# A layout of its own for the second expert pass in the weight ring of a two-layer decoder kernel

## The reference

```
logits = t @ w_router
top_v, top_i = lax.top_k(logits, TOP_K)            # 2 of 8
top_p = jax.nn.softmax(top_v, axis=-1)
combine = sum(one_hot(top_i, 8) * top_p[..., None], axis=1)
for e in range(8):
    out = out + combine[:, e:e+1] * ((silu(t @ w_gate[e]) * (t @ w_up[e])) @ w_down[e])
```

## Time and profile before

| what | us |
|---|---|
| median of 3 runs | 1017.01 (1016.84 to 1018.2) |
| the profiled execution | 1018.07 |
| its span | 1016.3 |
| TensorE busy in the span | 1001.5 (99%) |
| DMA, mean rate over the span | 250 GB/s (252.93 MB read) |

### The profile page before, as it was taken

The page is one execution under the profiler, slowest core; times in us unless marked ns, Lnnn a source line. Parts: engine busy times, 40 slices in busy tenths (PEclk is TensorE's granted clock), DMA queues, the critical chain, the costliest instruction groups (busy, mean ns, idle before and its releaser), DMA issues.

```text
span 1016.3 us, 22250 instructions
## 1 busy us (share of the span) xinstructions
PE 1001.5 (99%) x9679; PEld 863.3 (85%) x9679; DVE 592.1 (58%) x991; ACT 401.6 (40%) x627; POOL 13.6 (1%) x57
## 2 busy tenths in 40 slices
PE   8999999999999999999999999999999999999995
PEld 8999999999999999999999999996566566566552
DVE  6667766577677565376577665755542542542443
ACT  6735655535544344357356565352102002002012
POOL 3000000000000000000000000000000000000000
PEclk9999999999999999999999999999999999999998
DMA  7453543555555465465435437989979999999993
GB/s 282 160 159 104 198 146 111 187 200 189 176 187 186 144 217 201 150 232 166 163 107 188 154 99 263 394 326 405 405 305 414 410 411 414 413 408 414 414 408 139
DMA packets 56017, 255.40 MB, mean 251 GB/s; under 512 B 6609, under 2 KB 6641, under 8 KB 55922
## 3 DMA queue, kind: packets, MB, share of 16 engines
q1 hardware_dynamic: 55346, 252.94, 67.2%
q10 hardware_dynamic: 576, 1.07, 0.3%
HBM read 252.93 MB, written 1.05 MB: 250 GB/s over the span
## 4 chain that ended last, share of the span: by engine, by line
PE 85%; SPq 9%; DMA 3%; issue 1%; ACT 1%; DVE 1%; DVEq 0%
PE ps L1721 24%; PE ps L1716 18%; PE ps L1717 18%; PE ps L1718 18%; SPq L611 8%; PE ps L1710 2%; PE ps L1711 2%; PE ps L1712 2%; DMA e_ring<-in_experts 2%; DMA raw<-in_dense 1%; PE ps L1926 1%; ACT w_hi L754 0%; ACT squared L759 0%; PE ps L1744 0%; PE ps L1898 0%
## 5 line engine op out<-in xcount | busy, mean ns | idle before, releaser
L1075 DVE TENSOR_TENSOR w_lo<-raw,w_hi 128x1536 fp32r<-128x1536 f32 (+2 forms) x156 | 247.5, 1605 | 122.0 <-ACT w_hi L754 121.6
L754 ACT ACTIVATE w_hi<-raw 128x1536 fp32r<-128x1536 f32 (+2 forms) x156 | 209.2, 1362 | 145.2 <-DMA raw<-in_dense 142.5
L1716 PE MATMUL ps<-hT_hi,w_hi 128*128 128x256 f32 (+1 forms) x816 | 231.7, 284 | 1.6 <-DVE w_lo L1217 1.1
L1717 PE MATMUL ps<-hT_lo,w_hi 128*128 128x256 f32 (+1 forms) x816 | 230.4, 282 | 0.0
L1718 PE MATMUL ps<-hT_hi,w_lo 128*128 128x256 f32 (+1 forms) x816 | 229.6, 281 | 0.0
L1721 PE MATMUL ps<-e_ring,xe 128*32 128x352 f32 (+2 forms) x2480 | 186.5, 459 | 0.0
L1721 PEld LDWEIGHTS ps<-e_ring,xe 128*32 128x32 f32 x2480 | 109.8, 110 | 73.0 <-issue 32.3
L1716 PEld LDWEIGHTS ps<-hT_hi,w_hi 128*128 128x128 f32 (+1 forms) x816 | 152.2, 186 | 5.2 <-issue 2.6
L1717 PEld LDWEIGHTS ps<-hT_lo,w_hi 128*128 128x128 f32 (+1 forms) x816 | 152.3, 187 | 0.4
L1718 PEld LDWEIGHTS ps<-hT_hi,w_lo 128*128 128x128 f32 (+1 forms) x816 | 152.3, 187 | 0.4
L1717 PE MATMUL ps<-h_lo,w_hi 128*128 128x256 f32 x352 | 99.2, 282 | 0.0
(11 more groups left out here) (313 smaller groups left out, 1427.9 us busy)
## 6 DMA issues: line engine op xcount, KB each, us to landing
e_ring<-in_experts SPq DMA_DIRECT2D x124, 704.0 KB, 15.6
raw<-in_dense SPq DMA_DIRECT2D x112, 768.0 KB, 4.3
e_ring<-in_experts SPq DMA_DIRECT2D x88, 512.0 KB, 14.5
raw<-in_dense SPq DMA_DIRECT2D x42, 512.0 KB, 3.5
e_ahead<-in_experts SPq DMA_DIRECT2D x4, 704.0 KB, 9.1
raw<-in_dense SPq DMA_DIRECT2D x3, 544.0 KB, 4.9
raw<-in_dense SPq DMA_DIRECT2D x2, 272.0 KB, 4.2
x<-in_x SPq DMA_DIRECT2D x2, 256.0 KB, 4.5
```

The lines of the kernel that those rows point to most:

```text
L754: act.activation(slot(n, "hi", k), slot(n, "raw", k), ACT.Copy).then_inc(hi_done, 1)
L1075: dve.tensor_tensor(slot(n, "lo", k), slot(n, "raw", k), slot(n, "hi", k).bitcast(F32), ALU.subtract).then_inc(lo_done, 1)
L1716: pe.matmul(out, wh, hi, start=first, stop=False, skip_group_check=True)
L1717: pe.matmul(out, wh, lo, start=False, stop=False, skip_group_check=True)
```

## The change

The second pass gets a layout of its own, as the first has. `e_first_place` now takes the pass as its first argument (0 or 1) and names a buffer as well as a place.

- Pieces 0, 1 and 2 of the second pass go to the bottom of the first chunk, into the 5120 numbers that the first pass leaves empty (three large pieces take 4224 of them).
- Pieces 3 and 4 go to `e_ahead`, which held pieces 24 and 25 of the first pass.
- Pieces 5 to 23 go to the usual places of pieces 0 to 18.
- From piece 24 on, all go to their usual places.
- `e_first_before(i, u)` now returns the count of `e_used` itself: it looks through all earlier pieces, of this pass and the one before, for the last that lay in the same place.
- SyncE's program for passes 0, 1 and 2 is written out with constant waits, and its loop starts with the fourth pass. For the third pass the waits come to the same counts as before.
- TensorE reads the second pass's pieces from the new places (`turn` is passed through `hidden`, `down_main`, `down_over` and `down`). Which matmuls there are, and in which order, does not change.

```diff
+def e_first_place(i, u):
+
+    gate_up, size = 4 * 2 * KQ, 2 * HALF_E
+    shift = len(AHEAD) * size // D
+    if i == 0 and u in AHEAD:
+        return "ahead" + str(AHEAD.index(u) // 2), AHEAD.index(u) % 2 * size, size
+    if i == 0 and 24 <= u < gate_up:
+        return ("ring",) + e_place(u - len(AHEAD))
+    if i == 0 and u >= gate_up:
+        at = CHUNK_AT[0] + size * (gate_up - len(AHEAD) - 24) + D * (u - gate_up)
+        return ("ring",) + ((at, D) if at + D <= CHUNK_AT[0] + CHUNK else e_place(u - shift))
+    spare = shift * D // size
+    if i == 1 and u < spare:
+        return "ring", e_place(len(E_UNITS) - 1)[0] + size * u, size
+    if i == 1 and u < spare + 2:
+        return "ahead0", (u - spare) * size, size
+    if i == 1 and u < 24:
+        return ("ring",) + e_place(u - spare - 2)
+    return ("ring",) + e_place(u)
+
+def e_first_before(i, u):
+
+    buffer, at, size = e_first_place(i, u)
+    out = 0
+    for j in range(i + 1):
+        for v in range(u if j == i else len(E_UNITS)):
+            other, a, n = e_first_place(j, v)
+            if buffer == other and a < at + size and at < a + n:
+                out = max(out, j * E_GROUPS + E_GROUP[v] + 1)
+    return out
...
             for u in range(24 + len(AHEAD), len(E_UNITS)):
-                sp.wait_ge(e_used, E_GROUP[e_first_before(u)] + 1)
-                expert_load(u, (0, 1), first=True)
+                sp.wait_ge(e_used, e_first_before(0, u))
+                expert_load(u, (0, 1), 0)
             sp.wait_ge(route_ready, 1)
...
-            experts = [sp.value_load(ids[0:1, 2 + e:3 + e], min_val=0, max_val=NE - 1) for e in range(2)]
-            for u in range(len(E_UNITS)):
-                sp.wait_ge(e_used, E_GROUP[e_first_before(u)] + 1 if u < 24 else E_GROUPS + E_GROUP[e_before(u)] + 1)
-                expert_load(u, experts)
-            with sp.Fori(2, iters) as i:
+            for i in range(1, 3):
+                experts = [sp.value_load(ids[0:1, 2 * i + e:2 * i + e + 1], min_val=0, max_val=NE - 1) for e in range(2)]
+                for u in range(len(E_UNITS)):
+                    sp.wait_ge(e_used, e_first_before(i, u))
+                    expert_load(u, experts, i)
+            with sp.Fori(3, iters) as i:
```

More of the change, by code:

```diff
@@ L532, in load_of, with e_unit @@
             return loaded[n % RING], 16 * (n // RING + 1)
-        def e_unit(u, first=False):
+        def e_unit(u, turn=None):
             _, _, _, k, _, c = E_UNITS[u]
[L537 to L542, removed]
+            buffer, at, size = ("ring",) + e_place(u) if turn is None else e_first_place(turn, u)
+            home = {"ring": e_ring, "ahead0": e_ahead, "ahead1": eb["e_ahead2"]}[buffer]
+            return home[:, at:at + size].rearrange("p (k c) -> p k c", k=k)
         def proj_bank(n):
@@ L606, in load, with expert_load @@
                 sp.dma_start(unit(n, "raw", k, w), src).then_inc(load_of(n)[0], 16)
-            def expert_load(u, experts, first=False):
+            def expert_load(u, experts, turn=None):
                 which, e, k0, k, c0, c = E_UNITS[u]
                 src = block_of(t["experts"][experts[e]], expert_at[which, k0, k, c0, c], k, c)
-                sp.dma_start(e_unit(u, first), src).then_inc(loaded_e[u // 2], 16)
+                sp.dma_start(e_unit(u, turn), src).then_inc(loaded_e[u // 2], 16)
             free_later = {name: units for units, name in E_FREE_LATER}
@@ L2084, in quads, with hidden @@
                 return ins
-            def hidden(half, q, i, first=False):
+            def hidden(half, q, i, turn=None):
                 u = (half * KQ + q) * 4
-                units = [e_unit(u + n, first) for n in range(4)]
+                units = [e_unit(u + n, turn) for n in range(4)]
                 ks = (2 * q, 2 * q + 1)
@@ L2125, in slot_scales, with down_unit, down_main, down_over @@
                 ins.then_inc(scale_filled, 1)
-            def down_unit(k, e, first=False):
-                return e_unit(2 * KQ * 4 + 2 * k + e, first)[:, 0, :]
+            def down_unit(k, e, turn=None):
+                return e_unit(2 * KQ * 4 + 2 * k + e, turn)[:, 0, :]
             def down_ready(k, i):
                 expert_ready(2 * KQ * 4 + 2 * k, i)
-            def down_main(k, h, first=False):
+            def down_main(k, h, turn=None):
                 cols = slice(h * HALF, (h + 1) * HALF)
-                ins = quads(5 + h, HALF, ehT[:, k, :], [down_unit(k, e, first)[:, cols] for e in range(2)], k == 0, k == FET - 1)
+                ins = quads(5 + h, HALF, ehT[:, k, :], [down_unit(k, e, turn)[:, cols] for e in range(2)], k == 0, k == FET - 1)
                 if k == FET - 1:
                     ins.then_inc(y_filled, 1)
-            def down_over(ks, first=False):
+            def down_over(ks, turn=None):
                 for k in ks:
                     for g in range(4):
-                        ins = plain(ps[g * OV:(g + 1) * OV, 7, 0:QUARTER], ehT2[:, k, :], down_unit(k, 0, first)[:, g * QUARTER:(g + 1) * QUARTER],
+                        ins = plain(ps[g * OV:(g + 1) * OV, 7, 0:QUARTER], ehT2[:, k, :], down_unit(k, 0, turn)[:, g * QUARTER:(g + 1) * QUARTER],
                                     k == 0, k == FET - 1)
@@ L2149, in k_pair, with down @@
                 return range(2 * q, min(2 * q + 2, FET))
-            def down(q, i, first=False):
+            def down(q, i, turn=None):
                 for k in k_pair(q):
@@ L2157, in down, with first_half @@
                     for h in range(2):
-                        down_main(k, h, first=first)
+                        down_main(k, h, turn=turn)
                 if q == TURNED // 2:
                     pe.wait_ge(turn1_read, i * 2 + 2)
-                down_over(k_pair(q), first).then_inc(e_used, 1)
-            def first_half(i, first=False):
-                if not first:
+                down_over(k_pair(q), turn).then_inc(e_used, 1)
+            def first_half(i, turn=None):
+                if turn != 0:
                     pe.wait_ge(y_split, i * 3 + 3)
@@ L2171, in first_half, with second_half @@
                     slot_scales(i)
[L2172 to L2175, removed]
+                hidden(0, 0, i, turn)
+                hidden(0, 1, i, turn)
+                hidden(0, 2, i, turn)
+                if turn == 0:
                     pe.wait_ge(scale_known, 1)
                     slot_scales(i)
-                hidden(0, 3, i)
-            def second_half(i, first=False):
+                hidden(0, 3, i, turn)
+            def second_half(i, turn=None):
                 for q in range(KQ):
-                    hidden(1, q, i, first)
+                    hidden(1, q, i, turn)
                 pe.wait_ge(scale_ready, i + 1)
@@ L2190, in _, with full_pass @@
             pe.wait_ge(moe_zero, 1)
-            def full_pass(i, first=False):
-                first_half(i, first)
-                second_half(i, first)
+            def full_pass(i, turn=None):
+                first_half(i, turn)
+                second_half(i, turn)
                 for q in range(DQ):
-                    down(q, i, first)
+                    down(q, i, turn)
                 pe.wait_ge(sel_ready, i + 2)
@@ L2200, in _ @@
             for i in range(STATIC):
-                full_pass(i, i == 0)
+                full_pass(i, i)
             pe.wait_ge(iters_ready, 1)
```

## The result

The changed kernel takes 1019.56 us (median of 16 runs, 1017.92 to 1020.84) against 1017.33 (16 runs, 1016.4 to 1018.76): 2.2 us slower by the medians, ratio 1.0021 with the interval 1.0014 to 1.0029. The forecast was slower by 1.4 us, to 1018.4 us. The profiled execution has a span of 1017.1 us against 1016.3.

A forecast was written before the change was run, and what follows sets the result against it. The end was taken to follow the DMA stream's last landing, with at most 1.7 us to gain. New holes of 8.1 + 0.4 to 0.9 less 7.0, or +0.4 by landings, gave 1017.0 + 1.4 = 1018.4 us, range 1016.6 to 1019.9.

The forecast's parts named there:

- What bounds the kernel: Expert passes: the end follows the last DMA landing; earlier loads could gain at most 1.7 us, later ones cost fully.
- What the change gives: Start of the second pass: first issues come at about 732.6, and the 7.0 us DMA hole closes.
- What it takes: Second pass: piece 24 waits for count 16, not 15, a new 8.1 us hole; piece 27 adds 0.4 to 0.9.
- The sum: Whole kernel: holes opened less the hole closed, taken as +1.4 us, between +0.4 and +2.0.
- by landings: Pieces 24 and 27 of the second pass: landing times move by −0.2 and +0.4 us, so the end by +0.4.
- by the mean of the engines: DMA stream of the second pass: 8.1 + 0.4 to 0.9 − 7.0 = 1.5 to 2.0 us later.
- Edits at nothing: Other buffer for two DMAs, TensorE's weight reads, the third pass's counts and `ids` reads: no cost.
- The signs: Changed kernel's profile: empty windows at 779 to 785, last landing at 1000.5 to 1002.1, fourth TensorE down 26 to 28 us.
- The kept gain: Second pass: the old hole closes and no new one opens; −1.7 us, 1015.3 us; chance 4%.
- Landings rule: End of the loads: the slow engines are those forgiven at the hole; +0.2 to +0.7 us, about 1017.5; chance 28%.
- the forecast's own case: Whole kernel: slower by +0.8 to +2.0 us, 1017.8 to 1019.0 us; chance 46%.
- the rival with more holes: Second pass from piece 24: the queue runs short two or three times; +2.2 to +3.0 us, about 1019.6; chance 20%.

The follow-up runs named there:

- the longer wait: Kernel before, but piece 24 of the second pass waits for count 17 and not 15; ratio 1.0077 (1.0059 to 1.0095).
- the run with fewer bytes: Kernel before, but only the first half of pieces 24 to 31 of the second pass is loaded; ratio 0.9983 (0.9974 to 0.9992).
- the layout without the gap: Changed kernel with other places for pieces 24 to 53 of the second pass, and later counts in the third; ratio 0.9986, median 1015.8 us.
- the waits alone: Kernel before, but pieces 24 to 47 of the second pass wait for the changed kernel's counts; ratio 1.0024 (1.0013 to 1.0035).
- the late start: Changed kernel, but piece 0 of the second pass waits for count 8 again and not 6; ratio 1.0026 (1.0016 to 1.0036).
- the extra buffer: Kernel before, with pieces 3 and 4 of the second pass loaded to and read from another buffer, counts unchanged; ratio 0.9998 (0.9989 to 1.0007).

## Why the prediction was right, and where it was off

- *What bounds the kernel.* Right. TensorE's three first passes did not change in any run but the one with the longer wait, and the end moved with the DMA stream. The cap of 1.7 us is 1.8 us in the traces, and the run with fewer bytes shows it, which had 6.9 us of work less; the layout without the gap only just reaches it. One reading was incomplete: the 27th slice has 326 GB/s in the rows of before, so the 30th isn't the only exception. In windows of that trace the engines move 17 GB/s from 680 to 685 us, and are near 410 from 691 to 736. The queue is full from there to the hole at 737 us, so this earlier pause may well cost time too; no run tries it. It is there in the changed kernel too (39 GB/s from 680 to 685), so it doesn't bear on the difference.
- *What the change gives.* Right: the early issues came at 731.87, which is 732.7 on the time of the trace before, for a forecast of 732.6, and the hole of 7.0 us closed.
- *What it takes.* Right in place and cause: piece 24 waits for count 16, with all behind it. Its size was 7.8 us for 8.1, and 0.8 us at piece 27 for 0.4 to 0.9; no further hole opened. The run with the waits alone shows that this is the whole loss, within the noise.
- *The sum.* This is the term that was mis-sized. I took 1.4 us between +0.4 (by landings) and +2.0 (by the mean of the engines). The end by landings was wrong, though the two landings that it rests on came out as forecast: piece 24 landed at 789.3 on the time of the trace before (784.31 + 4.1 + 0.85) and piece 27 at 795.3. They are the first pieces behind each hole, and only these are early for their turn. Piece 28, right behind, landed 11.3 us after its issue at 785.16 before, at 796.5; in the changed kernel 6.4 us after its issue at 790.85, at 798.1 with the 0.85 us:

```profile
DMA to landing us min/median/max: 11.3/11.3/11.3
...
DMA to landing us min/median/max: 6.4/6.4/6.4
```

  That is 1.6 to 1.7 us later, not 0.4. The longer wait says the same: 6.8 us of hole became 6.9 us of time. The trace of the changed kernel has +1.6 us, and the medians 2.2, with an interval of 1.4 to 2.9 us. The three kernels with these waits have +1.6, +1.7 and +2.0 us in TensorE's fourth pass and +2.1, +2.6 and +2.4 us by the ratio. The intervals hold these sizes (that of the late start begins at 1.6 us), and single traces lie up to 0.4 us apart, so I can't say whether the half microsecond between is real; it stays open.
- *Edits at nothing.* Right for the extra buffer (0.9998). The written-out third pass of SyncE wasn't tried alone; the run with the waits alone had the loss without it, so there is no room for much.
- *The signs.* The forecast of 26 to 28 us for TensorE's fourth down part was wrong: it stayed at 25.79, and the delay came out in the gate and up groups before it. The sum of the pass is what tells. The last landing, forecast for 1000.5 to 1002.1, is at 1001.7 on the time of the trace before.
- *The rivals.* The kept gain would have needed engines still busy at 786; they ran dry at 778.0. *Landings rule* (+0.2 to +0.7 us, 28%) falls with the landings above and with the longer wait. By the traces the forecast's own case came true, in the upper half of its +0.8 to +2.0 us. By the medians it did not quite: +2.2 us, and 1019.56 us, are what the rival with more holes gave (+2.2 to +3.0, about 1019.6 us). But its mechanism isn't there: the start of piece 27 took the 0.8 us of the forecast's own case, and no third hole opened (407 GB/s from 793 to 820, as before from 800 to 820). The ratio of 1.0021 lies just beyond the 0.2% within which I put 71%, and its interval reaches to both sides. So the direction and the mechanism are earned. That 1.4 lies near the measured change is in part luck: it is a point between two ends of which one was wrong.

## What to carry to other kernels

When one in-order queue fills a ring, list for each transfer the count that frees its place, before and after, and date the counts from the trace: a layout that lets some pieces in earlier can make the first piece after the return to the old places wait longer, and everything behind it. The hole at 785 us, tried alone, was paid in full at the end, with the queue full behind it; the sums with the holes at 737 and 820 us fit the same rule, to some 0.4 us. So compare sums of holes, not single ones, and don't judge by the landing of the first piece behind a hole. And look for the floor at which another engine takes over: here it made 7 us less of DMA work worth 1.7.

## What I had not expected of the hardware

The first load behind a hole lands early for its turn, and the next ones don't. With the longer wait, piece 24 landed 5.8 us later than before, but piece 25 already 6.9 us later, and the end came 6.9 us later, for 6.8 us of hole by the mean rate. So the DMA engines' spread, which an empty queue seemed to forgive in that first landing, gave nothing back at the end. Why the spread is there again within one load of 704 KB no run here shows.
